# Swapping the halves of the rotary operands with a permutation matmul instead of two ScalarE copies

## The reference

```python
def rotary(t):                       # t: (B,H,L,d), d = 128
    d = t.shape[-1]
    l = t.shape[2]
    inv_freq = ROPE_BASE ** (-jnp.arange(0, d, 2, dtype=jnp.float32) / d)
    ang = jnp.arange(l, dtype=jnp.float32)[:, None] * inv_freq[None, :]
    cos, sin = jnp.cos(ang), jnp.sin(ang)
    tf = t.astype(jnp.float32)
    t1, t2 = tf[..., : d // 2], tf[..., d // 2:]
    return jnp.concatenate([t1 * cos - t2 * sin, t1 * sin + t2 * cos], axis=-1).astype(t.dtype)

def retention_branch(q_in, k_in, v_in, g_in, onorm_g):
    dk = BRANCH_W // RET_HEADS
    q = rotary(to_heads(q_in, RET_HEADS))
    k = rotary(to_heads(k_in, RET_HEADS)) * (dk ** -0.5)
    ...
    o = chunked_scalar_decay(q, k, to_heads(v_in, RET_HEADS), log_a)
    return group_rmsnorm(from_heads(o), onorm_g, RET_HEADS) * jax.nn.silu(g_in)
```

## Time and profile before

| | |
|---|---|
| runs | 3743.23, 3748.74, 3752.23 us; median 3748.74 |
| the profiled execution | 3743.23 us, span of the core 3741.4 us |
| TensorE busy, mean granted clock | 3565.5 us (95%), 0.979 |
| VectorE, ScalarE busy | 1945.5 us (52%), 1572.1 us (42%) |
| rotary units of layer 0 (woven with the core before) | about 2204 to 2410 us |
| rotary units of layer 1 | about 3334 to 3525 us |

### The profile page before, as it was taken

The page is one execution under the profiler, slowest core; times in us unless marked ns, Lnnn a source line. Parts: engine busy times, 40 slices in busy tenths (PEclk is TensorE's granted clock), DMA queues, the critical chain, the costliest instruction groups (busy, mean ns, idle before and its releaser), DMA issues.

```text
span 3741.4 us, 45121 instructions
## 1 busy us (share of the span) xinstructions
PE 3565.5 (95%) x18674; PEld 2865.4 (77%) x18674; DVE 1945.5 (52%) x2526; ACT 1572.1 (42%) x1826; POOL 90.8 (2%) x90
## 2 busy tenths in 40 slices
PE   7999999989999997999999999999999999999998
PEld 5787676866666665778888898788778888888777
DVE  4554453365565564556555563454465556663434
ACT  4332111255555553442446453433433456653432
POOL 0000000000000001000000000000000000000000
PEclk9999999999999998999999999999999999999999
DMA  5101351379999995122111011343122101011332
GB/s 197 46 26 51 126 183 62 121 278 366 370 370 367 367 373 222 43 67 78 46 51 52 23 74 46 112 147 131 50 74 68 49 32 51 35 57 46 127 127 102
DMA packets 95876, 487.53 MB, mean 130 GB/s; under 512 B 10753, under 2 KB 11265, under 8 KB 57777
## 3 DMA queue, kind: packets, MB, share of 16 engines
q1 hardware_dynamic: 77216, 417.31, 30.3%
q0 software_dynamic: 12688, 46.27, 3.4%
q10 hardware_dynamic: 5760, 20.97, 1.4%
HBM read 427.23 MB, written 57.28 MB: 129 GB/s over the span
## 4 chain that ended last, share of the span: by engine, by line
PE 51%; DVE 4%; ACT 4%; issue 2%; DMA 0%; DVEq 0%; ACTq 0%; POOLq 0%
PE ps L136 13%; PE ps L138 13%; PE ps L137 13%; PE ps L1737 3%; PE ps L1582 1%; PE ps L1562 1%; PE ps L1556 1%; PE ps L316 1%; PE ps L1525 1%; PE ps L1721 1%; PE ps L3490 1%; PE ps L3496 1%; PE ps L351 0%; PE ps L1502 0%; PE ps L359 0%
## 5 line engine op out<-in xcount | busy, mean ns | idle before, releaser
L136 PE MATMUL ps<-HH,WS 128*128 128x512 f32 (+1 forms) x2608 | 1044.4, 400 | 32.1 <-DVE WS L1339 21.9
L138 PE MATMUL ps<-HH,WS 128*128 128x512 f32 (+1 forms) x2608 | 1021.6, 392 | 0.0
L137 PE MATMUL ps<-HL,WS 128*128 128x512 f32 (+1 forms) x1968 | 771.4, 392 | 0.0
L136 PEld LDWEIGHTS ps<-HH,WS 128*128 128x128 f32 (+1 forms) x2608 | 492.6, 189 | 147.2 <-DVE WS L1339 25.7
L138 PEld LDWEIGHTS ps<-HH,WS 128*128 128x128 f32 (+1 forms) x2608 | 491.2, 188 | 106.8
L1402 ACT ACTIVATE WA<-ps 128x512 f32<-128x512 f32 x240 | 142.9, 596 | 821.4 <-PE ps L138 727.0
L137 PEld LDWEIGHTS ps<-HL,WS 128*128 128x128 f32 (+1 forms) x1968 | 372.4, 189 | 75.1 <-issue 1.0
L1339 DVE TENSOR_TENSOR WS<-RAW,WS 128x1024 fp32r<-128x1024 f32 (+1 forms) x153 | 200.4, 1311 | 167.2 <-ACT WS L1334 167.2
L136 PE MATMUL ps<-WS,HH 128*128 128x256 f32 x896 | 262.1, 292 | 12.6 <-DVE HL L2211 12.2
L138 PE MATMUL ps<-WS,HL 128*128 128x256 f32 x896 | 255.0, 285 | 0.0
L137 PE MATMUL ps<-WS,HH 128*128 128x256 f32 x896 | 255.0, 285 | 0.0
(11 more groups left out here) (399 smaller groups left out, 5282.7 us busy)
## 6 DMA issues: line engine op xcount, KB each, us to landing
WR<-in_weu SPq DMA_DIRECT2D x37, 1024.0 KB, 6.9
WR<-in_weg SPq DMA_DIRECT2D x35, 1024.0 KB, 8.3
WR<-in_wed SPq DMA_DIRECT2D x34, 1024.0 KB, 9.8
RAW<-in_wo SPq DMA_DIRECT2D x32, 1024.0 KB, 4.8
H<-in_wed SPq DMA_DIRECT2D x26, 1024.0 KB, 9.2
WA<-in_wada SPq DMA_DIRECT2D x48, 512.0 KB, 4.7
H<-in_weg SPq DMA_DIRECT2D x23, 1024.0 KB, 8.5
H<-in_weu SPq DMA_DIRECT2D x21, 1024.0 KB, 5.5
```

What stands on the lines that cost most here:

```text
L136: t.matmul(o, l[0], r[0], start=st, stop=False)
L137: t.matmul(o, l[0], r[1], start=False, stop=False)
L138: return t.matmul(o, l[1], r[0], start=False, stop=sp)
```

## The change

The swap becomes a matmul with a 0/1 permutation matrix `PERM` of 128x128, loaded once from DRAM on SP's queue behind `GK` (the wait of unit 2 for `GK` becomes one for `PERM`, loaded after it). The two 64-partition copies on ScalarE are gone; ScalarE's work on `u{z}` is a plain `scalar_project`. After each projection of `u{z}` TensorE multiplies each half of the copied tile `u` by `PERM` into a bank of its own (`perm`, line 1984), both halves after a wait for the copy of the second half. VectorE's product with the sines is now two instructions of 512 columns that read these banks, each after its own wait (`perm_mm`), and write tile `rs`. A projection's bank goes back on `copied` instead of `swapped`; tile `u` goes back after both the cosine product and the permutation; `ro` and `rs` are taken after the projection instead of around it. All matmuls that were there stay, in the same order.

```diff
--- before.py
+++ after.py
@@ -185,6 +185,7 @@
         MD = sb("MD", [128, 80])
         LB = sb("LB", [128, 12])
         GK = sb("GK", [16, 512])
+        PERM = sb("PM_", [128, 128])[:, :]
         bank_aps = [ctx.enter_context(nc.psum_tensor(f"ps{i}", [128, 512], F32))[:, :] for i in range(8)]
 
         h2d = nc.dram_tensor("h2_scratch", (1024, 1024), F32, kind="Internal").ap()
@@ -1961,11 +1962,12 @@
             if U % 2 == 0:
                 yield from plan_values(U)
             for z in range(2):
-                wa.take("u", U, z)
+                yield from plan_copied(U, f"u{z}", "u", U, z)
+                wa.take("ro", U, z)
                 wa.take("rs", U, z)
-                yield from plan_project(U, f"u{z}", lambda i: ("swapped", U, z, i))
-                wa.take("ro", U, z)
-                wa.give(("u", U, z), ("rcos", U, z))
+                for i in range(2):
+                    brief("perm", U, z, i, end=("rsin", U, z, i))
+                wa.give(("u", U, z), ("rcos", U, z), ("perm_mm", U, z, 1))
                 wa.give(("rs", U, z), ("rot", U, z))
             yield from plan_copied(U, "g0", "y", U, 0)
 
@@ -1974,19 +1976,20 @@
                 yield from tensor_values(t, U)
             for z in range(2):
                 yield from tensor_project(t, U, f"u{z}")
+                if U == 8:
+                    t.wait_ge(*at("small_in", "perm"))
+                for i in range(2):
+                    free(t, banks, "perm", U, z, i)
+                    t.wait_ge(*at("copied", "u", U, z, 1))
+                    t.matmul(ps("perm", U, z, i), PERM, half(tl("u", U, z), i), start=True, stop=True).then_inc(
+                        *up("perm_mm", U, z, i))
             yield from tensor_project(t, U, "g0")
 
         def scalar_prep_r(a, U):
             if U % 2 == 0:
                 yield from scalar_values(a, U)
             for z in range(2):
-                for i, _ in enumerate(scalar_project(a, U, f"u{z}", ("u", U, z))):
-                    b, s = ps("pj", *number(U, f"u{z}"), i), half(tl("rs", U, z), i)
-                    if i == 0:
-                        free(a, wa, "rs", U, z)
-                    a.activation(s[0:64, :], b[64:128, :], ACT.Copy)
-                    a.activation(s[64:128, :], b[0:64, :], ACT.Copy).then_inc(*up("swapped", U, z, i))
-                    yield
+                yield from scalar_project(a, U, f"u{z}", ("u", U, z))
             yield from scalar_project(a, U, "g0", ("y", U, 0), ACT.Silu)
 
         def vector_prep_r(v, U):
@@ -2001,9 +2004,11 @@
                 v.wait_ge(*at("copied", "u", U, z, 1))
                 free(v, wa, "ro", U, z)
                 v.tensor_tensor(o, tl("u", U, z), rc(U)[0], ALU.mult).then_inc(*up("rcos", U, z))
-                v.wait_ge(*at("swapped", U, z, 1))
-                v.tensor_tensor(s, s, rc(U)[1], ALU.mult).then_inc(*up("rsin", U, z))
-                v.wait_ge(*at("rsin", U, z))
+                free(v, wa, "rs", U, z)
+                for i in range(2):
+                    v.wait_ge(*at("perm_mm", U, z, i))
+                    v.tensor_tensor(half(s, i), ps("perm", U, z, i), half(rc(U)[1], i), ALU.mult).then_inc(*up("rsin", U, z, i))
+                v.wait_ge(*at("rsin", U, z, 1))
                 v.wait_ge(*at("rcos", U, z))
                 v.tensor_tensor(o, o, s, ALU.add).then_inc(*up("rot", U, z))
             yield
@@ -3654,7 +3659,7 @@
 
         def tensor_prep_g(t, U):
             layer, pr = U // 12, PLACE[U % 12]
-            t.wait_ge(*at("small_in", "gk"))
+            t.wait_ge(*at("small_in", "perm"))
             t.wait_ge(*at("dtrow", layer, 1))
             for i in range(2):
                 free(t, banks, "gk", U, i)
@@ -4185,6 +4190,7 @@
         def sync_program(s):
             mixer_sync(s)
             s.dma_start(GK[:, :], d["gk"]).then_inc(*up("small_in", "gk", by=16))
+            s.dma_start(PERM, d["perm"]).then_inc(*up("small_in", "perm", by=16))
             moe_sync(s)
             for layer in range(2):
                 layer_sync(s, layer)
@@ -4292,7 +4298,8 @@
         rot[2][:, 512 + h] = np.exp(lg * 128)
         rot[3][:, h * 128:(h + 1) * 128] = np.exp(lg * (t + 1))
         rot[3][:, 512 + h * 128:512 + (h + 1) * 128] = np.exp(lg * (127 - t)) * 128 ** -0.5
-    return ct, rm, lm.reshape(128, 448), rot
+    perm = (s == (t + 64) % 128).astype(np.float32)
+    return ct, rm, lm.reshape(128, 448), rot, perm
 
 
 def kernel(**inputs):
@@ -4312,8 +4319,8 @@
     def heads(w, offs, h):
         return fm(np.concatenate([w[:, o + h * 128:o + (h + 1) * 128] for o in offs], axis=1))
 
-    ct, rm, lm, rot = constants()
-    a = {"ct": ct, "rm": rm, "lm": lm, "rot": rot}
+    ct, rm, lm, rot, perm = constants()
+    a = {"ct": ct, "rm": rm, "lm": lm, "rot": rot, "perm": perm}
     a["xT"] = f["x"][0].T
     w = f["w_in"][0]
     a["w1p"] = np.stack([fm(w[:, 256 * i:256 * (i + 1)]) for i in range(2)])
```

## The result

The changed kernel takes 3788.56 us (median of 4 runs, 3785.25 to 3790.37), the kernel before 3747.9 us on the same chip (median of 4, 3743.23 to 3752.23): a ratio of 1.0108 with a 95% interval of 1.009 to 1.0126, so 40.7 us slower. The forecast was 3784.8 us. The profiled execution after took 3786.07 us around a span of 3784.3 us, which is 42.9 us more than the span before.

The account below looks back on a forecast made before the run. TensorE, busy for all of both rotary stretches, was taken as the only bound. Matmuls 27.4, waits 7.8 and restarts 0.8 sum to 36.0 us, added to the median 3748.74 for 3784.8 us; range 3770 to 3799.

Parts of the forecast that it names:

- ScalarE's 38 us: Rotary heads: the 32 pairs of swapping copies removed, 37.9 us, lie beside TensorE's stream and are worth 0.
- 32 matmuls at 1.71 a pair, 27.4 us: Rotary units on TensorE: added permutation matmuls, 16 pairs at the 1.71 us of a pair of L1582, cost 27.4 us.
- The lower bound from the rounded matmuls: Added permutation matmuls: 7.4 us if each went through in one go at 0.23 us.
- L933's 0.90: Added permutation matmuls, bound from above: L933 of the same shape takes 0.90 us each, so 28.8 us for 32.
- The wait, 7.8 us: TensorE between projection and permutation waits for ScalarE's copy of the second half: 7.8 us over both layers, bounds 0 and 15.0.
- the restart, 0.8: TensorE at the 8 bare places: the next projection half starts slowly, 0.1 us each, 0.8 us.
- the bare ones: Eight places over both layers with nothing between projection and permutation on TensorE, where 0.92 us of wait shows.
- VectorE, banks, tiles and the load, 0: Split sine product, later rotation, bank and tile returns and PERM's load on SP's queue: each 0, load at most 0.4 us.
- T + 4.7: End of VectorE's rotation at a bare place, T being when TensorE could start its next work; before, 4.5 us after T.
- The clock: Rival, rotary stretches: the 8 new holes lower TensorE's clock, 1.7 us each, 13.6 us more, 3798.4 us; chance 8%.
- VectorE late: Rival, rotary units: the rotation's slip of 1 us is wanted at every place, 16 us more, 3800.8 us; chance 5%.
- The swaps held the pipe: Rival, projection halves: the swaps had delayed TensorE by 1.2 us each, 38.4 us come back, 3746.4 us; chance 5%.

Follow-up runs that it names:

- no_swap: Kernel before without the two 64-partition copies and without any permutation, so the sine product reads unswapped u: 3745.13 us, ratio 0.9994.
- later: Changed kernel with both permutation matmuls of a pair issued behind the first half of the next projection: 3770.03 us, ratio 1.0066 to the kernel before.
- twice: Changed kernel with each permutation matmul issued twice into the same bank: 3811.79 us, ratio 1.0177 to the kernel before.
- rounded: Changed kernel with PERM and the copied q and k in the rounded format, losing low bits: 3762.35 us, ratio 1.0044 to the kernel before.
- wait_only: Kernel before with TensorE waiting for the second half's copy after each q and k projection, no permutation: 3755.61 us, ratio 1.0027.
- load_only: Kernel before with the permutation matrix loaded behind GK and waited for in unit 2, but unused: 3744.45 us, ratio 0.9992.
- again: The changed kernel measured once more without edit, beside the kernel before: 3785.65 us, ratio 1.0108.
- own_half: Changed kernel with each permutation matmul waiting only for the copy of its own half: 3775.32 us, ratio 1.0077 to the kernel before.

## Why the prediction was right

**TensorE is the bound, so ScalarE's 38 us are worth nothing.** Shown by no_swap: 196.77 us with and without the copies. The 37.9 us of the forecast came off ScalarE's busy time (38.6 measured) and off nothing else.

**32 matmuls at 1.71 a pair, 27.4 us.** Measured 27.0 (later) and 27.6 (twice). The row that was chosen, the same form from the same pool in another branch, was right to 2%. The lower bound from the rounded matmuls would have been right for other operands, which rounded shows; L933's 0.90 came from the lengths of records, which overlap.

**The wait, 7.8 us, and the restart, 0.8.** Together 8.6; wait_only measures 8.2, and taking the waits out of the change gives 9.4. By place: 0.94 us at the bare ones for 0.92, 0.15 behind the transposes for 0.12, and none behind the products. The count of the places, 8, 4 and 4, holds: the rows show eight waits. The restart can't be told apart so well. In wait_only it is 0.11 us. After a plain pair the next rounded matmul comes 0.41 us late, of which about 0.33 belong to the pair (1.72 us to the next start where nothing waits, 1.39 here) and 0.08 are left.

**VectorE, banks, tiles and the load, 0.** The rotation ended at T + 4.9 for a forecast of T + 4.7; later put it off further without a cost. load_only is at the time of before. One point of the last part of the prediction didn't show: VectorE was to be seen waiting at the halves of the sine product. It waits 1.4 us in all, since its cosine product (1.22 us) fills that time.

**The sum.** 36.0 us forecast, 36.4 in the stretches, 40.7 (33.7 to 47.2) in the medians, 38.4 in the second comparison (again). The mechanism is right, but the sum is closer than its terms: the matmuls were 0.4 us too high and the waits with their restarts 0.8 too low. How near 3784.8 (3748.74 + 36.0 is 3784.7) came to a median of 3788.56 is in part chance, as the interval of the measured difference reaches 6.7 us to either side and the forecast missed by 3.8.

**The rivals.** *The clock*: its mechanism would have shown a granted clock below 1.00 after the holes. It is 1.00 over both stretches of every kernel, and in every 5 us within them in the change and in wait_only, with eight holes of 0.94 us (the change) or 0.85 (wait_only). In layer 0 those of the change end at 2299.80, 2356.76, 2373.81 and 2417.16 us. So the rule of the Trainium skill that was weighed (TensorE: Matmul & The Clock Gate, "A second HAM failure mode: psum-queue depth-cycling") does not act on holes this short and this far apart.

But the ground that the prediction gave for it, the 1.00 after a wait of 2.1 us, held by the luck of one trace. In the tail of layer 0 of the kernel after, the same wait for ScalarE ends at 2439.92 us, and the clock falls behind it, before the next wait has begun; in the tail of layer 1 of the same trace the wait is as long and the clock stays. TensorE at both places, and windows of 5 us:

```profile
2439.92 2.69 PE L1526 MATMUL ps<-WA 128*128 128x128 f32 x14 [2.12 <-ACT WA L1510]
2446.94 3.29 PE L1563 MATMUL ps<-WA 128*128 128x128 f32 x14 [1.81 <-DVE WA L1541]
...
3572.02 1.80 PE L1526 MATMUL ps<-WA 128*128 128x128 f32 x14 [2.12 <-ACT WA L1510]
...
2440.00:2445.00 5.00, 5.00 (x30) 4.95 (x30) 4.90 (x7) 3.19 (x5) 0.00 (x0) 0.66 0.88 288
2445.00:2450.00 5.00, 3.19 (x16) 2.77 (x15) 2.82 (x8) 0.60 (x1) 0.00 (x0) 0.75 0.85 326
...
3572.00:3577.00 5.00, 3.59 (x30) 3.42 (x30) 4.90 (x7) 3.29 (x5) 0.00 (x0) 1.00 0.92 286
```

Of the 20 such waits (two tails in each of ten traces) eight are followed by some 3 us at the lower level, and two of the eight stand in kernels without a permutation or an added wait (layer 1 of no_swap and of load_only). So it is not shown to be the change's doing. Nor does it cost time there: the next group but one (L1563, L1562 before) starts 11.96 us behind the scores in the kernel before (2421.07 - 2409.11) and in the one after (2446.94 - 2434.98), as it waits for VectorE in both. Holes of about 2 us in place of the 0.94 might have made the rival come true; no run here has them in a stretch that TensorE bounds.

*VectorE late* falls with later. *The swaps held the pipe* falls with no_swap, whose gain of 0.7 us can't be told from none (its interval reaches from 5.6 us faster to 1.1 slower).

**What stays open.** The opening of the first trace after was 6.8 us slower to the issue of `GK` than that of before. In the other eight traces this issue lies at 716.1 to 721.1 us, with and without parts of the change; the code there is the same in all. The traces tie the difference to the granted clock: ordered by the issue, the clocks of the three hundreds are 0.95, 0.95, 0.97 (before and later, 716.1), 0.95, 0.97, 0.91 (again 718.1, no_swap 718.6), 0.93, 0.97, 0.91 (rounded 719.3, load_only 719.8), 0.93, 0.95, 0.91 (twice and wait_only 720.8, own_half 721.1) and 0.93, 0.93, 0.91 (after, 722.9). In each of the first four groups stand kernels with and without the permutation. That the clock's level there is chance from one execution to the next is what again suggests, with one more trace of the same kernel; it was not shown by many traces of one kernel. The four traces without any permutation matmul (before, no_swap, load_only, wait_only) have 716.1, 718.6, 719.8 and 720.8 there, the six with it 716.1, 718.1, 719.3, 720.8, 721.1 and 722.9; an effect of a microsecond or two can't be excluded.

## What to carry to other kernels

Work taken off an engine that nobody waits for has no value, and the same work given to the engine that is busy for the whole stretch costs its full price, here 27 us for a function that ScalarE did beside it for nothing. Ask first for the busy share of the stretch, not of the kernel. Where TensorE must multiply what another engine just copied out of its own bank, the bill has two parts: put as much of its own work between the two as the hole is long, here 0.94 us, or let the first half start on its own copy, and look at the format of the operands, since a plain f32 matmul of 128x512 took 0.86 us and a rounded one 0.23.

## What the runs showed that was not expected

A stretch bounded by TensorE at clock 1.00 repeats to about 0.01 us from one execution to the next, and from layer to layer (214.97 four times, 196.77 or 196.76 in the kernel before, no_swap and load_only), while the ratios of the medians are known to 3 to 7 us. Two kernels with holes differ more between the layers: wait_only by 0.09 us (200.92 and 200.83) and rounded by 0.07 (205.02 and 204.95); why stays open. Even so an effect of a microsecond in such a stretch could be told from one trace each, where the times alone could not.

The opening, in contrast, differs between traces of one kernel with equal busy time: of its ten microseconds from 110 us on TensorE is busy in all ten in both the traces of the changed kernel, at a granted clock of 0.64 in the first and 0.83 in the second:

```profile
110.00:120.00 10.00, 10.00 (x53) 7.06 (x52) 2.25 (x8) 7.69 (x9) 0.00 (x0) 0.64 0.01 2
```
```profile
110.00:120.00 10.00, 10.00 (x58) 8.09 (x58) 4.59 (x11) 7.29 (x9) 0.00 (x0) 0.83 0.01 2
```

And the first rounded matmuls behind a plain f32 one start 0.64 us apart, where two rounded ones behind a rounded permutation keep their 0.23: part of what the plain matmul costs shows only behind it (which part of the array's work that is, no run shows), so a group's cost is read to the second start after it.
